# Layer norm in token layout: residual as a PSUM seed instead of identity matmuls, normalising over three engines

## The reference, cut to what matters

```python
# first block, twice
mix = merged @ w_out[l]                       # merged: gated sum of retention and two attentions
x = layer_norm(ALPHA * x + mix, ln1_g[l], ln1_b[l])
ffn = (silu(x @ w_gate) * (x @ w_up)) @ w_ffn_out[l]
x = layer_norm(ALPHA * x + ffn, ln2_g[l], ln2_b[l])
# second block, twice
x = layer_norm(ALPHA * x + 0.5 * swiglu(x, ffn1...), ln1_g, ln1_b)
proj = x @ w_in[l]                            # convolution, gated MLP and sparse attention read it
x = layer_norm(ALPHA * x + concat(y_a, y_b, y_c) @ w_out[l], ln2_g, ln2_b)
x = layer_norm(ALPHA * x + 0.5 * swiglu(x, ffn2...), ln3_g, ln3_b)
```

## Time and profile before

| | |
|---|---|
| runs | 2027.08, 2028.13, 2028.14 us |
| profiled execution | span 2026.5 us from the first to the last instruction, 1.6 us under the median of the runs; no separate time for it is shown |
| granted clock, mean | 0.999 |
| DMA | 352.5 MB in all, 174 GB/s |
| VectorE, ScalarE, GpSimd busy | 63%, 46%, 2% |

### The profile page before, as it was taken

How to read it: one execution, slowest core, us unless ns; L and a number is a source line. 1 busy time by engine, 2 the same in 40 slices (tenths; PEclk the granted TensorE clock), 3 DMA queues, 4 the chain that set the end, 5 groups by cost and what they waited for, 6 DMA issues and landing times.

```text
span 2026.5 us, 32504 instructions
## 1 busy us (share of the span) xinstructions
PE 2010.1 (99%) x14176; PEld 1838.1 (91%) x14176; DVE 1274.6 (63%) x1844; ACT 927.4 (46%) x1275; POOL 32.2 (2%) x56
## 2 busy tenths in 40 slices
PE   8999999999999999999999999999999999999998
PEld 7888999999887999999999989799999998979997
DVE  6566666555756665655665567765566556776555
ACT  4445444443545444544444454454444445445442
POOL 0000000000000000000000000000000000000000
PEclk9999999999999999999999999999999999999999
DMA  8543555666554556496556646458656664545663
GB/s 287 167 151 132 187 169 170 196 207 190 167 163 138 166 167 186 144 266 187 167 177 189 189 134 167 103 158 252 187 167 187 188 188 133 160 135 158 188 190 101
DMA packets 416133, 352.51 MB, mean 174 GB/s; under 512 B 28816, under 2 KB 361080, under 8 KB 415992
## 3 DMA queue, kind: packets, MB, share of 16 engines
q1 hardware_dynamic: 415992, 350.44, 57.3%
HBM read 349.36 MB, written 1.05 MB: 173 GB/s over the span
## 4 chain that ended last, share of the span: by engine, by line
PE 94%; DVE 3%; ACT 2%; issue 0%; DMA 0%; DVEq 0%; SPq 0%
PE ps L201 29%; PE ps L203 29%; PE ps L202 29%; PE ps L1446 2%; PE ps L1527 2%; PE ps L1565 1%; DVE hl L1990 1%; PE ps L1599 1%; ACT hl L1749 1%; DVE er L2157 0%; DVE small L2116 0%; ACT er L1841 0%; PE ps L1637 0%; DVE er L2114 0%; PE ps L1570 0%
## 5 line engine op out<-in xcount | busy, mean ns | idle before, releaser
L1990 DVE TENSOR_TENSOR hl<-raw,hl 128x1024 fp32r<-128x1024 f32 (+2 forms) x555 | 756.3, 1393 | 393.4 <-ACT hl L1749 392.4
L201 PE MATMUL ps<-xt,hl 128*128 128x256 f32 (+1 forms) x2672 | 753.9, 282 | 0.0
L202 PE MATMUL ps<-xt,hl 128*128 128x256 f32 (+1 forms) x2672 | 746.2, 279 | 0.0
L203 PE MATMUL ps<-xt,hl 128*128 128x256 f32 (+1 forms) x2672 | 745.9, 279 | 0.0
L1749 ACT ACTIVATE hl<-raw 128x2048 fp32r<-128x2048 f32 (+1 forms) x323 | 613.2, 1900 | 182.8 <-PE ps L203 169.5
L201 PEld LDWEIGHTS ps<-xt,hl 128*128 128x128 f32 (+1 forms) x2672 | 501.0, 187 | 4.6 <-issue 1.5
L202 PEld LDWEIGHTS ps<-xt,hl 128*128 128x128 f32 (+1 forms) x2672 | 501.1, 188 | 3.1
L203 PEld LDWEIGHTS ps<-xt,hl 128*128 128x128 f32 (+1 forms) x2672 | 500.8, 187 | 0.2
L201 PE MATMUL ps<-hl,o 128*128 128x512 f32 x656 | 261.5, 399 | 0.0
L203 PE MATMUL ps<-hl,o 128*128 128x512 f32 x656 | 259.0, 395 | 0.0
L202 PE MATMUL ps<-hl,o 128*128 128x512 f32 x656 | 258.8, 394 | 0.0
(11 more groups left out here) (202 smaller groups left out, 1606.5 us busy)
## 6 DMA issues: line engine op xcount, KB each, us to landing
raw<-in_w_in SPq DMA_DIRECT2D x83, 1024.0 KB, 5.1
raw<-in_w_ffn_in SPq DMA_DIRECT2D x88, 512.0 KB, 5.1
raw<-in_ffn_gate SPq DMA_DIRECT2D x88, 512.0 KB, 4.1
raw<-in_ffn_up SPq DMA_DIRECT2D x88, 512.0 KB, 5.3
raw<-in_ffn_down SPq DMA_DIRECT2D x44, 1024.0 KB, 5.1
raw<-in_w_ffn_out SPq DMA_DIRECT2D x22, 1024.0 KB, 5.0
raw<-in_w_out SPq DMA_DIRECT2D x12, 1024.0 KB, 5.1
raw<-in_w_branch_a SPq DMA_DIRECT2D x8, 1024.0 KB, 4.9
```

Source lines behind the costliest of these rows:

```text
L201: e.matmul(out, l[0], r[0], start=start, stop=False)
L202: e.matmul(out, l[0], r[1], start=False, stop=False)
L203: return e.matmul(out, l[1], r[0], start=False, stop=stop)
L1990: e.tensor_tensor(lo[:, c], m["raw"][:, k % NRAW, 0:n][:, c], hi[:, c].bitcast(F), ALU.subtract).then_inc(s.low.up(("low", k), *([("low", ...
```

## The change

In words: X now holds the finished x in token layout. The sums of each norm are seeded: ScalarE copies x into the PSUM bank, and all products, the first too, accumulate onto it (`mm3_onto`). `ai` and `residual` go. A seed needs a bank whose columns were all written by matmuls since they were last cleared, so banks carry a mark `dense`, `Ring.take` can ask for one, and a bank shared by two products now has one start flag instead of two. g and b come as broadcast rows (`rows_in`, four DMAs of 512 columns onto 128 partitions for each norm, into `et`, or into `rt` and half of `sg` for norms 6 and 9). The affine on transposed tiles, its columns in the staging and `last_in` go.

Places: the seeds of the first block stand before the last merge unit, those of the out products in the second block where its residual stood, those of a net after its first two units and after its third. `rows_in` stands in a net after its fourth unit, in the first block in the third merge, and for norms 6 and 9 right behind `layer_norm` of norms 5 and 8.

```diff
+def mm3_onto(e, out, l, r):
+    e.matmul(out, l[0], r[0], start=False, stop=True, skip_group_check=True)
...
     def in_halves(pieces):
+        turn, split = P.half
         pieces(0, 0, (0, 1))
+        pieces(1, 0, (0,))
+        turn(0)
+        pieces(1, 0, (1,))
+        turn(1)
+        split()
         P.prep_next()()
         pieces(0, 1, (0, 1))
         pieces(1, 1, (0, 1))
...
     def layer_norm(acc, tail, final=False):
...
+        stats(0)
         if final:
             for t in tail:
                 t()
+            stats(1)
             return
         for t in tail[:3]:
             t()
         low = P.prep_next()
-        turn(0)
+        turn(0, 0)
         tail[3]()
-        rest()
-        affine(0, lambda: low(2))
+        turn(0, 1)
+        low(2)
+        split(0)
         stats(1)
         low(2)
...
+    def seed(b, i, c):
+        dense([b])
+        add("seed", b, i, c, ("xn", P.xv, i, c) if P.xv else ("x", i))
...
+        layer_norm(acc, tail)
+        rows_in(I["ln2_g_2"][l], I["ln2_b_2"][l], [RT.take() for _ in range(2)] + [Place(...)  for c in range(2)])
...
 (SP)
+    def rows_in(srcs, places, v):
+        for src, x in zip(srcs, places):
+            e.wait_ge(*T[x.before])
+        e.wait_ge(*T["rows read", v - 1] if v > 1 else (None, 0))
+        for src, x in zip(srcs, places):
+            e.dma_start(x.ap, src.partition_broadcast(128)).then_inc(s.rows.up(("rows", v)), 16)
...
 (ScalarE)
+    def ln_norm(i, acc, small, rows, v, out="xn"):
+        x = X[:, i, 512:1024]
+        e.wait_ge(*T["rs", v, i])
+        e.wait_ge(*T["scaled by g", v, i])
+        e.activation(x, x, ACT.Copy, scale=small[2]).then_inc(done.up(("normalised", v, i)), 1)
+    def ln_split(i, banks, v):
+        for q, b in enumerate(banks):
+            e.wait_ge(*T[b.full])
+            e.activation(XT[:, 0, 4 * q:4 * q + 4, ...], b.ap..., ACT.Copy)...
+    def seed(b, i, c, x_event):
+        e.wait_ge(*T[x_event])
+        e.wait_ge(*T[b.before])
+        e.activation(b.ap, X[:, i, c * 512:(c + 1) * 512], ACT.Copy).then_inc(done.up(b.seed), 1)
...
 (GpSimd)
+    def ln_norm(i, acc, small, rows, v, out="xn"):
+        x = P.m["x"][:, i, 512:1024]
+        e.wait_ge(*T["normalised", v, i])
+        e.wait_ge(*T[out, v, i, 0])
+        e.tensor_tensor(x, x, rows[3].ap, ALU.add).then_inc(done.up((out, v, i, 1), *([("rows read", v)] + ... if i else [])), 1)
...
 (VectorE)
+    def ln_norm(i, acc, small, rows, v, out="xn"):
...
+        for c in range(2):
+            e.scalar_tensor_tensor(X[:, i, c * 512:(c + 1) * 512], acc[c].ap, mv[:, 0:1], rows[c].ap, ALU.subtract, ALU.mult)...
+        x = X[:, i, 0:512]
+        e.wait_ge(*T["rs", v, i])
+        e.wait_ge(*done.now)
+        e.scalar_tensor_tensor(x, x, rs, rows[2].ap, ALU.mult, ALU.add).then_inc(done.up((out, v, i, 0)), 1)
+    def ln_split(i, banks, v):
         for c in range(4):
+            e.wait_ge(*T["xt high", v, i, c // 2])
+            e.tensor_tensor(lo, quarter(banks, c), hi.bitcast(F), ALU.subtract)...
```

More of the change, by code:

```diff
@@ L520, in proj_t, with first_units @@
         return t_unit(*t_proj(*args, **kw))
-    def first_units(two, more):
+    def first_units(two):
         P.ahead = 1
@@ L525, in first_units, with rows_in, row_slots, layer_norm @@
         us = [P.unit(segs, UNIT) for segs in two]
-        bs = [PB.take() for _ in two]
+        bs = dense([PB.take() for _ in two])
         def pieces(n, i, parts):
             for p in [q for p in parts for q in (2 * p, 2 * p + 1)]:
-                add("first_piece", us[n], bs[n], i, p, xt_i(v, i, p), p == 0 and i == 0, p == 3, i == 1 and p == 3)
-        in_halves(pieces, more)
-        return bs
-    def layer_norm(acc, gb, gb_event, tail, final=False):
+                add("first_piece", us[n], bs[n], i, p, xt_i(v, i, p), p == 0 and i == 0, p == 3 and i == 1)
+        in_halves(pieces)
+        return bs
+    def rows_in(g, b, places):
+        P.rows = places
+        add("rows_in", [x[c * 512:(c + 1) * 512] for x in (g, b) for c in range(2)], places, P.xv + 1)
+    def row_slots():
+        return [ET.take() for _ in range(4)]
+    def layer_norm(acc, tail, final=False):
         v = P.xv
-        def rest():
-            for c in range(2):
-                add("residual", acc[1][c], 1, c, [], False, [("xt read", v, 1)] if c else [])
+        rows, P.rows = P.rows, None
         P.xv += 1
@@ L574, in layer_norm, with acc_pair @@
         low = P.prep_next()
-        turn(0)
+        turn(0, 0)
         tail[3]()
-        rest()
-        affine(0, lambda: low(2))
+        turn(0, 1)
+        low(2)
+        split(0)
         stats(1)
         low(2)
[L581 to L587, removed]
+        for x in rows:
+            if x.ring is ET:
+                ET.give(x)
+            elif x.ring is RT:
+                RT.give(x)
+        P.half = (lambda q: turn(1, q), lambda: split(1))
+    def seed(b, i, c):
+        dense([b])
+        add("seed", b, i, c, ("xn", P.xv, i, c) if P.xv else ("x", i))
+    def acc_pair(i=None, c=None):
+        pair = [PB.take(True), PB.take(True)]
+        for n, b in enumerate(pair):
+            seed(b, *((i, n) if c is None else (n, c)))
+        return pair
     def out_part(w, acc, src_events, c, r=0, ks=(0, 2)):
@@ L653, in dn @@
                 P.tick()
[L654 to L660, removed]
+        for j, b in enumerate(first_units([gate_up(0), gate_up(1)])):
             up(j, b, True)
-        acc.append([PB.take(), PB.take()])
+        acc = [acc_pair(i=0)]
         up(2)
+        acc.append(acc_pair(i=1))
         up(3)
+        rows_in(g, b_, row_slots())
         for d in range(9):
@@ L2087, in ffn_gate, with ln_last @@
+    def ln_last(i, acc, small, rows, v):
+        ln_norm(i, acc, small, rows, v, "last")
     def ffn_gate(b, th, tm, n, scale):
```

288 lines of the change are left out of this document (110 added, 178 removed).

## The result

The changed kernel takes 2051.12 us (median of 4 runs, 2050.49 to 2051.46) against 2028.14 for the kernel before (4 runs): a ratio of 1.0115, 95% interval 1.0103 to 1.0127. It is slower by 23.0 us; forecast were 4.9, with 2043 as the upper end of the range.

What follows compares the result with a forecast made beforehand. TensorE, busy 99% of the span, was taken to bound the kernel. -35.0 + 24.3 + 11.0 + 4.0 + 0.6 = +4.9 us on 2028.13 gave 2033.0 us, range 2017 to 2043.

Steps and rivals of the forecast that it cites:

- the seeds: 40 ScalarE copies into PSUM, costed at nothing because a slack of 1.3 us in a net covers them; bound +7.
- the bank order: A clause within the 0.40 case of slower by 4 to 9: another bank order may cost more than seen; no price.
- Residual matmuls, norm waits: Twenty batches of residual matmuls leave TensorE, -35.0 us; new TensorE waits in the windows of norms 1 to 9, +24.3 us.
- the walk: Step-by-step timing of norm 5: TensorE waits 0.35, 1.25, 0.85 and 0.75 us, together 3.2 us.
- GpSimd's add: Add of b for each tile's second half: 1.25 us; in tile 1 it starts only when VectorE's low half ends.
- The third unit: Behind norms 5 and 8 its load queues on SP behind the row request: TensorE waits 5.5 us, twice, +11.0 us.
- The clock: TensorE's granted clock falls after each 5.5 us wait: 2.0 us each time, +4.0 us, bounds 0 and 4.
- The other four [batches]: Residual batches ahead of the two kinds of out products, outside the norm windows; their removal was taken as pure gain.
- The end: Tile 1's last half goes through three engines, 1.35 us after its first half instead of 0.75: +0.6 us.
- The faster one: Rival, chance 0.20: the row request behind norms 5 and 8 doesn't delay the third unit's load; 2018 us.
- slow add: Rival: GpSimd's add takes 3 us, kernel 2052 us; chance 0.15 for both slower-still cases together.
- lock first: Rival: GpSimd's add gets the lock before VectorE's low half, delaying it 1.25 us; 2044 us; shares the 0.15 chance.

Runs made afterwards that it cites:

- run 2: Changed kernel, with the request for the g and b rows of norms 6 and 9 no longer waiting for the read of the rows before: 2029.65 us.
- run 5: Changed kernel, with tile 0's first seed in the second block's out products moved between last score pair and exponentials, weave order behind the seeds restored: 2047.24 us.
- run 7: Changed kernel with the row request's wait removed and one seed early for each of the two pairs in the second block's out products: 2025.02 us.
- run 10: Changed kernel with the row request's wait removed and tile 0's residual matmuls back in the second block's out products, tile 1 still seeded: 2025.13 us.
- run 12: Run 2's edit on the changed kernel, plus both tiles' residual matmuls instead of seeds in the second block's out products, any bank allowed: 2019.26 us.

## Why the prediction was wrong

The direction was right; the size was about a fifth of what came (4.9 of 23.0), and the range to 2043 didn't reach it. The step that failed is the seeds, costed at nothing where nothing was looked up; with them goes the bank order, which had no price. By its own steps:

- **Residual matmuls, norm waits.** -35.0 and +24.3. Right in mechanism, outside the second block's out products. In the seven plain stretches together -8.5 was measured against -5.8 forecast; if the batches are taken as priced, the windows were priced 0.4 too high each, which makes some 21 in all. No run parts the two terms. In norm 5 TensorE waited 0.23, 0.96, 0.41 and 0.48 where the walk had 0.35, 1.25, 0.85 and 0.75: the same four waits in the same order. From the root to the first product of tile 1 it is 13.64 us (1190.43 to 1204.07) against 12.90 before, 0.74 longer where the walk had 1.0. One count is off by one, without effect on the sum: fifteen batches stood inside the windows, not sixteen; the other is norm 10's at the end.
- **GpSimd's add.** 1.25 forecast, 1.29 alone. In tile 1 it took 2.14, from 1201.16 to 1203.30, while VectorE's low part ran from 1200.94 to 1202.16: so it is as the walk had it, 1.14 behind the end of that. The Trainium skill's "GPSIMD Engine Reference", section 3.1, gave an estimate of 1.12; the measured one stands.
- **The third unit.** +11.0, measured 15.4. Right mechanism, one term undersized: the load was to reach ScalarE's high part 5.6 us after its issue behind the rows, and took 7.7 (1205.19 to 1212.89) and 8.5, inside its bounds of 5.1 and 9. The fourth unit's load went out 0.5 us behind it (1205.67), so how much of this is the rows and how much the next load is not shown.
- **The clock.** +4.0; what run 2 gave back beyond the waits is 6.1, above the bound of 4. In the trace, the changed kernel was 1.7 us behind at the end of the rest of norm 5 and 4.4 at 1235: 2.7 for one of the two.
- **"Seeds ... I cost the seeds at nothing."** This step failed. Its cover was looked up in a feed-forward net and held there. In the second block's out products nothing was looked up, and the seed stands behind the exponentials: the first product waited 4.07 for it, and with the waits and the half clock behind it the place behind norm 5 lost some 6.4. Seeds queued earlier take that wait away (runs 5 and 7); run 7 is 4.6 us faster than run 2.
- **"The other four [batches] ... are pure gain."** For the two of the second block, 3.5 us, that is not borne out: run 7 without these 32 matmuls and run 10 with them, under the same rule for banks, take the same time (2025.02 and 2025.13), while in the profiled executions run 7's two stretches are 0.5 and 2.0 shorter. So their removal was worth 0 to 2.5 us, and they partly filled rests, as far as these two runs tell: the compressed scores waited 2.00 in run 7 and 1.16 in run 10. But their absence is not what made the loss.
- **The loss in the out products, summed.** In run 2, where the third unit isn't late, the two stretches are still 6.7 and 6.2 us longer than before, where the terms give -0.75: 14.5 us. With the third unit's 6.5 (waits and clock) and -2.8 of the seven plain stretches that is 18.2, and 18.1 were missing.
- **Bank order.** The prediction named it in one clause, as part of its own case and with no price. Run 12 against run 10 puts it, with tile 1's seed, at some 3.7 us for a block, even with 16 matmuls more.
- **The end.** +0.6; the tail from norm 10's root for tile 0 to the last instruction is 0.87 shorter (12.77 to 11.90), with a batch of 1.75 gone from it: +0.9.
- **The rivals.** The faster one, third unit not late, is run 2: but it gave 2029.65, not 2018, since the out products' loss was in none of the cases. The slower ones (slow add, lock first) didn't happen; their 2044 to 2052 would have been reached for a wrong reason.

The part before norm 1 can't be read: its root starts between 310.1 and 311.9 in runs whose code is the same up to there.

## What to carry to other kernels

Work on the engine that bounds the kernel can be filling: before it is counted as gain, look at each place where it stands and ask what the engine would wait for without it, in every kind of stage and not in one. Here 3.5 us of such work were worth 0 to 2.5. A start value that moves from the bounding engine to a helper should be queued on the helper ahead of the work that would hold it up, and it pins banks: price the takers that it drives into other banks. A wait in a load queue costs only at the place where the queue reaches it, so a request should stand behind the event it waits for by more than the number of loads that run ahead.

## What was unexpected of the hardware

- The granted clock fell after two short rests: in run 10 TensorE rested for 1.16 us up to 1288.13 and for 0.99 up to 1289.51, and the clock was 0.84 from 1288 to 1290 and 0.50 from 1290 to 1296. In run 12, without these rests, it stayed at 1.00 from 1288 to 1292.
- The releaser that the profile names was wrong for the new wait of 4.07 us ("DVE hl L2001"): in run 5, with the seed queued earlier, the same product started 1.95 us before that low part.
- A 1 MB load issued directly behind 1 MB of broadcast rows took 7.7 and 8.5 us to its first reader, against a median of 5.1 us from issue to landing. The next load was issued 0.5 us behind it, and the runs don't part the two.
